# One kernel, two network blocks on one core: one chain for two stacked norms, context norm moved, decay columns first, weight low halves in four pieces

## What is computed

```
h = first_block(x)                      # ... h = h + conv_glu_ffn(rmsnorm(h, ffn_norm[1]))
h = rmsnorm(h, final_norm)              # norm 1: y1 = h * r1 * g1, r1 = rsqrt(mean(h*h) + eps)
xn  = _modulate(_rms(h, norm_attn), shift, scale)        # norm 2, on the 512 tokens
ctx = _modulate(_rms(ctx, norm_attn), shift_c, scale_c)  # norm 2, on 256 context tokens
proj = [xn, ctx] @ w_in                 # q,k,v (3072), beta and decay logits (32), gates ...
q,k,v = silu(centred_conv5(qkv)); g = -exp(a_log) * softplus(decay + dt_bias); beta = sigmoid(...)
... gated delta rule, second attention, gates from xn, merge, MLP
```

## Time and profile before

| what | us |
|---|---|
| median of 3 runs (range) | 3008.35 (3007.01 to 3008.8) |
| the profiled execution, its own time | 3009.29 |
| its span in the trace | 3007.5 |
| TensorE busy in the span | 2720.5 (90%) |
| VectorE, GpSimd, ScalarE busy | 1719.9, 929.1, 636.8 |
| granted TensorE clock, mean over the span | 0.948 of full |

### The profile page before, as it was taken

The page is one execution under the profiler, slowest core; times in us unless marked ns, Lnnn a source line. Parts: engine busy times, 40 slices in busy tenths (PEclk is TensorE's granted clock), DMA queues, the critical chain, the costliest instruction groups (busy, mean ns, idle before and its releaser), DMA issues. The chain is left out here.

```text
span 3007.5 us, 44742 instructions
## 1 busy us (share of the span) xinstructions
PE 2720.5 (90%) x18637; PEld 2232.4 (74%) x18637; DVE 1719.9 (57%) x2471; ACT 636.8 (21%) x1217; POOL 929.1 (31%) x332
## 2 busy tenths in 40 slices
PE   7989999998889999486899879978899899989998
PEld 6768888776668888475898779865556688768887
DVE  6858668664478577566455555533433725575371
ACT  3221011102222011233443254301133210010000
POOL 2424343343134444222221232111100344334443
PEclk9989999999989999698999989989799999989999
DMA  3224343220024343110101101101000122222222
GB/s 145 88 94 147 118 141 125 106 84 29 32 109 139 121 154 110 52 65 22 31 31 57 43 23 38 44 21 34 28 1 1 61 95 97 84 84 98 98 96 72
DMA packets 45649, 226.88 MB, mean 75 GB/s; under 512 B 5056, under 2 KB 6816, under 8 KB 26912
## 3 DMA queue, kind: packets, MB, share of 16 engines
q1 hardware_dynamic: 45472, 224.32, 21.4%
HBM read 222.16 MB, written 2.15 MB: 75 GB/s over the span
## 5 line engine op out<-in xcount | busy, mean ns | idle before, releaser
L235 POOL TENSOR_TENSOR ring_rounded<-ring,ring_rounded 128x2048 fp32r<-128x2048 f32 (+4 forms) x190 | 783.5, 4124 | 1381.2 <-DVE ring_rounded L230 1381.2
L254 PE MATMUL psum<-arena_rounded,ring_rounded 128*128 128x512 f32 (+2 forms) x2820 | 1097.4, 389 | 71.7 <-DVE arena_rounded L1513 17.6
L255 PE MATMUL psum<-arena_rounded,ring_rounded 128*128 128x512 f32 (+2 forms) x2820 | 1090.2, 387 | 0.0
L256 PE MATMUL psum<-arena_rounded,ring_rounded 128*128 128x512 f32 (+2 forms) x2820 | 1089.0, 386 | 0.0
L254 PEld LDWEIGHTS psum<-arena_rounded,ring_rounded 128*128 128x128 f32 (+1 forms) x2820 | 536.4, 190 | 188.6 <-issue 69.6
L230 DVE CAST ring_rounded<-ring 128x2048 fp32r<-128x2048 f32 (+4 forms) x191 | 214.1, 1121 | 709.6 <-PE psum L256 652.9
L255 PEld LDWEIGHTS psum<-arena_rounded,ring_rounded 128*128 128x128 f32 (+1 forms) x2820 | 536.8, 190 | 106.8 <-issue 1.5
L256 PEld LDWEIGHTS psum<-arena_rounded,ring_rounded 128*128 128x128 f32 (+1 forms) x2820 | 535.7, 190 | 107.6
L665 ACT ACTIVATE arena<-psum,vectors 128x512 f32<-128x512 f32 x88 | 68.5, 781 | 409.1 <-PE psum L256 409.1
L295 DVE CAST arena_rounded<-arena 128x512 fp32r<-128x512 f32 (+2 forms) x113 | 135.0, 1195 | 9.2 <-DVE arena L2738 0.8
L2096 DVE TENSOR_TENSOR arena<-psum,lev 128x256 f32<-128x256 f32 x120 | 49.9, 423 | 105.9 <-PE psum L1867 103.4
(11 more groups left out here) (356 smaller groups left out, 3195.1 us busy)
## 6 DMA issues: line engine op xcount, KB each, us to landing
ring<-in_w_up SPq DMA_DIRECT2D x44, 1024.0 KB, 4.8
arena<-in_w_mod SPq DMA_DIRECT2D x48, 512.0 KB, 3.4
ring<-in_w_down SPq DMA_DIRECT2D x32, 704.0 KB, 4.0
ring<-in_w_mup SPq DMA_DIRECT2D x16, 1024.0 KB, 4.8
ring<-in_w_mdown SPq DMA_DIRECT2D x16, 1024.0 KB, 4.8
ring<-in_w_gdn SPq DMA_DIRECT2D x12, 1024.0 KB, 4.8
ring<-in_w_lru_in SPq DMA_DIRECT2D x10, 1024.0 KB, 4.8
ring<-in_w_odd_in SPq DMA_DIRECT2D x10, 1024.0 KB, 4.8
```

Of the source, the lines that this page charges most:

```text
L235: pool.tensor_tensor(self.rounded(self.ring[:, 2, slot, 0:seg.size]), self.ring[:, 0, slot, 0:seg.size], self.rounded(self.ring[:, 1, slot ...
L254: pe.matmul(out, r(wh), r(xh), start=start, stop=False)
L255: pe.matmul(out, r(wh), r(xl), start=False, stop=False)
L256: return pe.matmul(out, r(wl), r(xh), start=False, stop=stop)
```

## The change

1. **One chain for the two norms.** `renorm_stage` and `norm2_stage` are gone. While the second feed-forward adds its last half to `h`, ScalarE also squares `h * g1` and VectorE sums it into a second accumulator (`Residual` with `gained`). `gdn_in_stage` for heads 0 to 3 starts with `SecondNorm`: sums of both accumulators (8 columns), r1, then r2, then the two spreads of r1*r2 and of r1; the scaled `h` for the residual is made by `dve_residual` behind the norm.
2. **The context is normed in the odd output stage** (`odd_out_stage`, long before), under the matmuls of that stage; its rounding is done in `SecondNorm` (`context(k)`), and GpSimd copies it once for the second group of heads.
3. **Unit `bd` comes first** in the order, and k units come before q units. The products of `bd` and of the first unit with the context stand ahead of and between the spreads; the decay chain is spread over the gaps after units 1, 2 and 3.
4. **`merge_stage` uses the kept r2** (`known`) and starts with the spread.
5. **The low half of a unit is made in four pieces** (two for 513 to 1024 columns), by instructions of their own.
6. In `lru_stage` x is loaded ahead of the small constants, and ScalarE runs one small `Square` before it waits for x.

The core of the diff:

```diff
     def split_lo(self, pool, seg, slot, g):
         pool.wait_ge(self.hi_done, g + 1)
-        pool.tensor_tensor(self.rounded(self.ring[:, 2, slot, 0:seg.size]), self.ring[:, 0, slot, 0:seg.size],
-                           self.rounded(self.ring[:, 1, slot, 0:seg.size]).bitcast(F32),
-                           ALU.subtract).then_inc(self.lo_done, 1)
+        pieces = 4 if seg.size > 1024 else 2 if seg.size > 512 else 1
+        for i in range(pieces):
+            raw, high, low = [self.ring[:, part, slot, i * seg.size // pieces:(i + 1) * seg.size // pieces]
+                              for part in range(3)]
+            last = pool.tensor_tensor(self.rounded(low), raw, self.rounded(high).bitcast(F32), ALU.subtract)
+        last.then_inc(self.lo_done, 1)
...
+def norm_stage_parts(m, acc, gain, xh, xl, shift=None, known=None):
...
     def pe_part(pe):
-        rstd_pe_sums(m, pe, acc, 4, 7)
-        pe.wait_ge(m.sem("rstd"), m.count("rstd", 1))
-        rstd_pe_spread(m, pe, root, 4, lambda i: m.psum[:, 6, i * P:(i + 1) * P])
+        if known is None:
+            rstd_pe_sums(m, pe, acc, 4, 7)
+            pe.wait_ge(m.sem("rstd"), m.count("rstd", 1))
+        rstd_pe_spread(m, pe, root if known is None else known, 4, lambda i: m.psum[:, 6, i * P:(i + 1) * P])
...
         ins = dve.tensor_tensor(self.acc, self.acc, self.sq[:, slot, :], ALU.add)
+        if self.gained:
+            ins = dve.tensor_tensor(self.acc2, self.acc2, self.sq2[:, slot, :], ALU.add)
...
+            ins = act.activation(self.acc if first else self.sq[:, slot, :], pick(m.h, tile), ACT.Square)
+            if self.gained:
+                ins = act.activation(self.acc2 if first else self.sq2[:, slot, :], pick(m.h, tile), ACT.Square,
+                                     scale=col(self.gained[0], tile))
...
         m.load(sp, *m.units[0], 0)
-        for view, src in first:
-            sp.dma_start(view, src).then_inc(m.up("vectorsin", 16), 16)
         for i in range(4):
             sp.dma_start(m.h[:, 2 * i:2 * i + 2, :], x[:, 2 * i:2 * i + 2, :]).then_inc(m.up(f"xin{i}", 16), 16)
+            if i == 0:
+                sp.dma_start(vectors[0], vectors[1]).then_inc(m.up("vectorsin", 16), 16)
+        for view, src in first:
+            sp.dma_start(view, src).then_inc(m.up("unitsin", 16), 16)
...
-        act.wait_ge(m.sem("vectorsin"), m.count("vectorsin", 16 * len(first)))
+        act.wait_ge(m.sem("halves"), m.count("halves", 1))
+        act.activation(m.small[:, 287:288], m.small[:, S_HALF:S_HALF + 1], ACT.Square).then_inc(m.achain.up(), 1)
+        act.wait_ge(m.sem("vectorsin"), m.count("vectorsin", 16))
...
+def odd_out_stage(m, seg, v, ctx):
...
+    def sp(sp):
+        sp.dma_start(xc, ctx.rearrange("(k p) t -> p k t", p=P)).then_inc(m.up("ctxin", 16), 16)
...
+            if unit.u == 0:
+                pe.wait_ge(m.sem("csummed"), m.count("csummed", KD - 1))
+                rstd_pe_sums(m, pe, acc, n, 7)
+            if unit.u == 1:
+                pe.wait_ge(m.sem("rstd"), m.count("rstd", 1))
+                rstd_pe_spread(m, pe, root, n, lambda i: m.psum[:, 6, i * P:(i + 1) * P])
...
+        add_bias(m, dve, v, slice(0, MODS_READY))
+        gain_dve(m, dve, gain, v["norm_attn"], m.mods[:, KD:2 * KD, 1])
+        for k in range(1, KD):
+            dve.wait_ge(m.sem("csquare"), m.count("csquare", k + 1))
+            dve.wait_ge(m.sem("csummed"), m.count("csummed", k - 1))
+            dve.tensor_tensor(acc, acc, sq[:, k % 2, :], ALU.add).then_inc(m.up("csummed"), 1)
+        res.dve_unit(dve, us[0])
+        dve.wait_ge(m.sem("ssq"), m.count("ssq", 1))
+        rstd_dve_mean(m, dve, m.psum[:, 7, 0:n], mean, 1.0 / D)
+        dve.wait_ge(m.sem("root"), m.count("root", 1))
+        rstd_newton(m, dve, mean, root, tmp, m.sig("rstd"))
+        res.dve_unit(dve, us[1])
+        dve.wait_ge(m.sem("spread"), m.count("spread", 1))
+        for k in range(KD):
+            dve.scalar_tensor_tensor(xc[:, k, :], xc[:, k, :], col(gain, k), m.psum[:, 6, 0:TC],
+                                     ALU.mult, ALU.mult).then_inc(m.up("cnormed"), 1)
+        for unit in us[2:]:
             res.dve_unit(dve, unit)
+        res.dve_end(dve)
+    def pool(pool):
+        rstd_pool(m, pool, mean, half, root, 1)
+        for unit in us:
+            m.pool_unit(pool, unit)
...
+class SecondNorm:
...
+    def pool(self, pool):
+        m = self.m
+        rstd_pool(m, pool, self.mean, self.half, self.r1, 1)
+        rstd_pool(m, pool, self.mean2, self.half, self.r2, 2)
+        pool.tensor_copy(self.xn[:, :, CTX], self.xc).then_inc(m.up("ctxkept"), 1)
+    def act(self, act):
+        m = self.m
+        for k in range(KD):
+            act.activation(m.rounded(self.xh[:, k, CTX]), self.xc[:, k, :], ACT.Copy).then_inc(m.up("chigh"), 1)
+        for k in range(KD):
+            x = self.xn[:, k, 0:T]
+            act.wait_ge(m.sem("xnormed"), m.count("xnormed", k + 1))
+            act.activation(x, x, ACT.Identity, bias=m.mods[:, k, 0:1]).then_inc(m.up("xshifted"), 1)
+            act.wait_ge(m.sem("xshifted"), m.count("xshifted", k + 1))
+            act.activation(m.rounded(self.xh[:, k, 0:T]), x, ACT.Copy).then_inc(m.up("xhigh"), 1)
+            if k == 1:
+                act.wait_ge(m.sem("spread"), m.count("spread", 2))
...
+        add_bias(m, dve, self.v, slice(MODS_READY, 48))
+        gain_dve(m, dve, self.gain, self.v["norm_attn"], m.mods[:, KD:2 * KD, 0])
+        dve.tensor_tensor(self.gain, self.gain, self.v["final_norm"], ALU.mult).then_inc(c.up(), 1)
+        dve.wait_ge(m.sem("ssq"), m.count("ssq", 1))
+        rstd_dve_mean(m, dve, m.psum[:, self.sums, 0:NT], self.mean, 1.0 / D)
+        context(0)
+        dve.wait_ge(m.sem("root"), m.count("root", 1))
+        rstd_newton(m, dve, self.mean, self.r1, self.tmp, m.sig("rstd"))
+        dve.wait_ge(m.sem("rstd"), m.count("rstd", 1))
+        dve.tensor_tensor(self.tmp, self.r1, self.r1, ALU.mult).then_inc(c.up(), 1)
+        dve.wait_ge(c.sem, c.now())
+        dve.tensor_tensor(self.tmp, self.tmp, m.psum[:, self.sums, NT:2 * NT], ALU.mult).then_inc(c.up(), 1)
+        dve.wait_ge(c.sem, c.now())
+        rstd_dve_mean(m, dve, self.tmp, self.mean2, 1.0 / D)
+        context(1)
+        context(2)
+        dve.wait_ge(m.sem("root"), m.count("root", 2))
+        dve.wait_ge(m.sem("mean"), m.count("mean", 2))
+        rstd_newton(m, dve, self.mean2, self.r2, self.tmp, m.sig("rstd"))
+        dve.wait_ge(m.sem("rstd"), m.count("rstd", 2))
+        dve.tensor_tensor(self.r12, self.r1, self.r2, ALU.mult).then_inc(m.up("rootprod"), 1)
+        for k in range(3, KD):
+            context(k)
+        dve.wait_ge(m.sem("spread"), m.count("spread", 1))
+        for k in range(KD + 1):
+            if k < KD:
+                dve.scalar_tensor_tensor(self.xn[:, k, 0:T], m.h[:, k, :], col(self.gain, k), m.psum[:, self.b12, :],
+                                         ALU.mult, ALU.mult).then_inc(m.up("xnormed"), 1)
+            if k:
+                low(k - 1)
+    def dve_residual(self, dve):
+        m = self.m
+        dve.wait_ge(m.sem("r1row"), m.count("r1row", 1))
+        for k in range(KD):
+            dve.scalar_tensor_tensor(m.h[:, k, :], m.h[:, k, :], col(self.v["final_norm"], k), self.r1row,
+                                     ALU.mult, ALU.mult).then_inc(m.vchain.up(), 1)
+        dve.wait_ge(m.vchain.sem, m.vchain.now())
...
+        first = us[0]
+        if bd:
+            norm.pe_sums(pe)
+            pe.wait_ge(m.lo_done, bd.g + 1)
+            for k in range(KD):
+                pe.wait_ge(m.sem("cready"), m.count("cready", k + 1))
+                rows(k, 1)
+            pe.wait_ge(m.lo_done, first.g + 1)
+            pe.wait_ge(m.sem("mean"), m.count("mean", 2))
+            for t in range(2):
+                for k in range(KD):
+                    tile(first, t, k, 1)
+                norm.pe_spread(pe, t)
+            for k in range(KD):
+                pe.wait_ge(m.sem("xready"), m.count("xready", k + 1))
+                last = rows(k, 0)
+                if k == KD - 1:
+                    last.then_inc(m.up("bdrows"), 1)
+                last = tile(first, 0, k, 0)
+            last.then_inc(m.up("done"), 1)
+            for k in range(KD):
+                last = tile(first, 1, k, 0)
+            last.then_inc(m.up("done"), 1)
...
+            if unit.u == 1:
+                pe.wait_ge(m.sem("bdcopied"), m.count("bdcopied", 2))
+                for i in range(NA):
+                    last = pe.transpose(bdb[:, i, :], bdt[:, i * P:(i + 1) * P], m.ident[0:32, 0:32])
+                last.then_inc(m.up("bdturned"), 1)
+            if unit.u == 2:
+                pe.wait_ge(m.sem("decays"), m.count("decays", 1))
+                g = n3(cols(GG))
+                for d in range(2):
+                    pe.matmul(m.psum[:, 6, 48 * d:48 * d + 48], m.cum[:, d, :], g[:, :, 8 * d:8 * d + 8],
+                              start=True, stop=True)
```

(25 more changed lines are left out.)

321 lines of the change are left out of this document (159 added, 162 removed).

## The result

The changed kernel takes 2964.0 us (median of 4 runs, 2950.2 to 2967.1) against 3008.6 (3007.0 to 3009.2): the ratio is 0.984, 95% interval 0.981 to 0.988. The profiled execution took 2964.4 us, its span is 2962.6, so the spans of the two profiles differ by 44.9.

What follows compares the result with a forecast made beforehand. The time is TensorE's work plus the places where it stands still. Terms -26.6 - 3.6 - 1.2 + 1.4 - 0.6 + 2.0 = -28.6 off the median 3008.35 give 2979.7, say 2980; range 2968 to 2992.

Steps and rivals of the forecast that it cites:

- The stretch from A: From the second feed-forward's last down matmul to the token stage: 152.9 us against 179.0, so -26.1.
- loses 1.7 more at the lower clock: In-projection, after TensorE idles 2.8 us for the second unit's low half: some eight matmuls at twice 0.227.
- loses about 2.5 at the lower clock: In-projection, after TensorE idles 7.1 us for the decays: same estimate after a longer hole.
- The alternation: GpSimd pieces and VectorE instructions take turns, at the feed-forward's end and with the residual multiplies; read from the branch stage.
- rival 1: Overlap closer to complete: pieces run unbroken, copy loses its turn, first stage's Newton step gets through; -40, 2968; chance 0.14.
- Rival 2: Decays' unit first buys little: the decay wait moves but doesn't shrink, 12 to 15 us go back, 2992 to 2995; chance 0.09.
- The small terms: Outside the large stretch: merge -3.6, first stage -1.2, odd output +1.4, odd in-projection -0.6, stage ends and a late bank +2.0.
- -1.2: First stage: -3.2 for the earlier start, +2.0 for four Newton holds and a cold restart; bounds -5.6 and +1.
- -0.6: Odd in-projection: three waits for low halves shift by -1 to +2.6 and partly cancel.
- +2.0 in all: Stage ends with a low half running (+0.5 first feed-forward, +1.1 attention heads) and a late bank in group two's third narrow unit.
- The four holds of the Newton step: First stage: four dependent Newton instructions, held once for 4.55 us, are held once each by pieces; TensorE idles some 4.7 us.
- The rule on the ports: First to issue holds the shared ports for its whole instruction; splitting wins nothing for dependent small instructions: +2.0, not -3.3, first stage.

Runs made afterwards that it cites:

- e11: Changed kernel with GpSimd's copy of the context moved behind the low half of the unit after the next: 2968.0 us.
- e5: Changed kernel with the eight residual multiplies moved behind the third unit's taps: 2966.1 us.
- e12: Changed kernel with low halves in eight pieces for units over 1024 columns, four for those over 512: 2965.6 us.
- e3: Changed kernel with the decays, cumulative sums and turn of the rows back behind the last unit, the decays' unit still first: 2967.8 us.
- e2: Changed kernel with each low half in one instruction as before: 2964.9 us.
- e1: Kernel before with only the low halves made in four pieces: 3003.8 us, ratio 0.997.
- f1: Kernel before with 14 unread filling products at the end of TensorE's part of the heads' norm stage: 2999.8 us.
- e6: Changed kernel with the cumulative sums behind the fourth unit and the turn of the rows behind the fifth: 2953.0 us.
- e8: Changed kernel with units in the order keys, values, queries in both groups: 2952.0 us.
- e10: Changed kernel with later residual multiplies, sums and context copy, order keys, values, queries, and 14 filling products: 2929.7 us, ratio to the kernel before 0.975.

## Why the prediction was right in kind and short in size

**The stretch from A: right in its steps, 7.4 us too long.** Point by point, with the prediction's A, B (the stage's start) and E (the end of the loop over k), from the traces. The stage starts at A + 8.5 (9.5 was forecast): an add and a piece take 1.7 us as a pair, not 1.27 + 0.67 = 1.94. The product of the roots is ready 10.2 us later (12.2), and the last spread ends 22.6 us later (25.3): the copy of the context held the Newton step for 1.7 us, where 2.4 were taken, and the three subtracts that were put ahead of the roots fit under them. From there to the last spread it is 12.4 us (13.1, where the prediction's own terms add to 12.6). The second low half came at E + 7.6 us (8.3), TensorE idled 2.12 (2.8). The decays came 18.8 us behind the second unit (19.0), with a hole of 7.27 (7.1), and the last taps took 12.48 (12.5). The terms that were too large: about 1.0 us for the stage's start, 2.7 for the chain, 0.7 for the low half, and 3.1 for the clock, the largest. The step that failed there is "loses 1.7 more at the lower clock" and "loses about 2.5 at the lower clock". Behind the 2.12 us the granted clock stayed at 1.00 (the window of after beside e11), and the narrow unit behind the decays took 12.3 us, 1.4 more than the 10.9 at the full clock; with the sums ahead of it that is 1.4 less than forecast. The alternation that the prediction took from a single place was right: e5, e12 and the rows of the pieces show it, and rival 1, in which GpSimd ran unbroken, did not happen, though its time did.

**The early decay chain is not where the gain came from.** The prediction didn't part the norm from the decays. e3 does: the early chain is worth 0.8 us. Of the stretch's 33.5 us, 26 are the 57 us at 0.52 that became 30.9 at 0.67, that is, the chain of the two norms with work laid under it. The other 7.5 lie behind: the full products took 98.5 us and take about 91 now, since the context's products of the decays' unit and of the first unit have already run in the 30.9. What it is worth that the decays' unit is first, and gives a third of these products, no run tells. Rival 2 (the decay wait moves but doesn't shrink) was right in that moving the wait buys little, and wrong in its price: the wait was the 7.27 us of the forecast and not 12.94, and no 12 to 15 us went back.

**The pieces: priced as a loss, a gain of 8.5 us outside the stretch (e2: 2.9, 4.3 and 1.3) against 2.9 in it.** The step that failed, and the larger part of the miss, is "The small terms": "-1.2" for the first stage, "-0.6" for the odd in-projection and "+2.0 in all" at stage ends. The four holds of the Newton step are as forecast (idle 5.08, forecast 4.7). What was left out is that a VectorE instruction freed of a long hold brings forward the root behind it and so the next low half: -3.9 in the odd in-projection (e1 alone: -3.8). In the merge it is plainer: TensorE's last wait for VectorE's low half of an activation (L297, L300) fell from 2.96 to 1.58 us (e2, then after), -1.3. In the first stage each half alone gave 1.0 and 1.2 us (e1, e2) and both 4.1. Part of the difference is the clock: in e2, with the new start alone, the last waits of TensorE come 2.4 us earlier than in before (the last at 148.47 and 150.90 us), and 1.2 are lost behind them, where the granted clock of the next 12 us is 0.75 against 0.86. With that, the parts give 1.0 and 2.4; the rest, 0.7 us, is no more than the stage moved between before and f1 (191.5 and 192.2), which are alike in it. The 5.5 us that the two groups, the latent projections and the rest gave beyond the forecast are not traced to the change.

**The rule on the ports held, both ways.** In the rows a Newton instruction lasts as long as the GpSimd instruction that started just ahead of it, 1.2 or 0.7 us, and four of them in a row pay four times. The Trainium skill, page SBUF — State Buffer, section Who interferes with whom, says that the first to issue has the shared ports for its whole instruction; by that rule the trace agrees. What the prediction made of it was too narrow: four pieces win nothing for a chain of dependent small instructions (one hold of 4.5 against four of 1.2), but eight do (four holds of 0.67), and four win for a single large one (4.20 became 0.94). In that paragraph the sum is off too: 2.0 and 3.3 off 2979.7 give 2974.4, not 2974.7.

**The clock of the heads' stage: not forecast.** 5.4 us of the profile against the change, up to 15 between traces of kernels that are alike in that stage. Without it the forecast would have been off by more: -47 to -50 against -28.6.

What stays open: why executions of the same kernel differ in that stage (three of thirteen traces escaped the cold stretch), and how much of the 1.3 and 2.6 us in the two groups is the change. The runs show +/-2 there with no edit in them.

## What to carry to other kernels

A low half that stands beside VectorE's large two-input instructions was worth splitting here, and the right size differs by place: small pieces where VectorE's chain is awaited, whole ones where GpSimd's result is. Before spreading a chain to hide it, count what covers it: here a chain of 18.8 us stood over a unit of 10.9, and moving its use one unit on closed the hole (e6), while putting the narrow units last shortened the last wait (e8). When a term of a few us is read, compare stretches of the trace, since a clock that falls in a stage the edit doesn't touch can be larger than the term. In the changed kernel the gain of the pieces shows in that way only.

## What the runs showed of the hardware

- A stretch at the lower clock of 20 to 31 us (10 to 15 us of time) came behind a hole of 2.36 us in ten of thirteen traces without the filling (not in e1, e3 and e12), and in none of four with 14 thin products in the hole. Behind the hole of 2.11 to 2.14 us ahead of the second unit, a short one came in one of seven traces (e11, clock 0.86 in the next 12 us; after, 1.00).
- Gains ahead of such places can be partly taken back: e5 and e11 closed 1.8 and 1.7 us of holes and got 1.0 and 0.5. In e10, without the hole ahead of the second unit, e11's edit gained 2.4 us.
- A row of VectorE adds and a row of GpSimd pieces, both queued, take turns: a pair takes 1.7 us where the parts alone take 0.67 and 1.27.
- A GpSimd copy of 128x2048 took 1.88 us where a subtract with two inputs of that size took 4.62, and held VectorE as long.
